# Expert weights in pairs of slabs with 16 KB per partition, and late small loads, in a four-layer block kernel

## The reference

```python
def first_block(x, c, ...):                 # d = 1024, s = 512
    mod = silu(c) @ w_ada + b_ada           # six vectors of 1024
    h = rmsnorm(x) * (1 + sc1) + sh1
    u_f, q, k, v = split(h @ w_in)          # fourier part, 8 query heads, 2 key heads
    y_f = fourier_mix(u_f)                  # 2-D FFT, real part, per-head matrix
    y_a = windowed_gqa(rmsnorm(q), rmsnorm(k), v, rel_bias, sink)
    x = x + g1 * (concat(y_f, y_a) @ w_out)
    h2 = rmsnorm(x) * (1 + sc2) + sh2
    return x + g2 * expert_choice_moe(h2)   # 16 experts, 64 tokens each

def expert_choice_moe(h, w_router, w_gate, w_up, w_down):
    aff = softmax(h @ w_router)
    g, idx = top_k(aff.T, 64)               # each expert picks its tokens
    y = (silu(xin @ w_gate) * (xin @ w_up)) @ w_down   # all 1024 x 1024, per expert
    return scatter_add(g * y, idx)
```

## Time and profile before

| | |
|---|---|
| median of 3 runs | 2066.1 us (2063.94 to 2067.38) |
| the profiled execution | 2064.61 us, span 2062.8 us |
| PE busy | 1986.6 us, 96% of the span |
| DVE, ACT, POOL busy | 906.0, 703.9, 14.0 us |
| mean granted TensorE clock | 0.987 of 2.4 GHz |
| moved by DMA | 344.13 MB, of which the experts' weights are 201 MB |

### The profile page before, as it was taken

One profiled execution on the slowest core, in us unless ns is written; L12 is line 12 of the kernel. 1 busy time (PEld: TensorE's weight loads), 2 busy tenths in 40 slices (PEclk: granted clock), 3 DMA queues, 4 the chain that ended last, 5 costly groups with the idle time before them and its releaser, 6 DMA issues.

```text
span 2062.8 us, 23302 instructions
## 1 busy us (share of the span) xinstructions
PE 1986.6 (96%) x9639; PEld 1310.7 (64%) x9639; DVE 906.0 (44%) x1371; ACT 703.9 (34%) x1171; POOL 14.0 (1%) x28
## 2 busy tenths in 40 slices
PE   5999999999999899999999999999998899999999
PEld 4755543333333257775488887877787568888787
DVE  3474132211111145463266666335545447666433
ACT  4354211111111042473333333235443544333323
POOL 1000000000000000000000000000000000000000
PEclk9999999999999999999999999999999999999999
DMA  9459259999999961400233322221212014333221
GB/s 316 149 191 300 80 229 421 422 421 421 421 421 421 421 198 33 143 1 17 65 82 102 101 84 101 93 92 62 82 62 62 1 41 123 90 95 102 84 80 41
DMA packets 180844, 344.13 MB, mean 167 GB/s; under 512 B 21275, under 2 KB 143755, under 8 KB 152963
## 3 DMA queue, kind: packets, MB, share of 16 engines
q1 hardware_dynamic: 179120, 340.46, 45.7%
q0 software_dynamic: 944, 1.91, 0.5%
q10 hardware_dynamic: 675, 0.27, 0.1%
HBM read 340.50 MB, written 2.11 MB: 166 GB/s over the span
## 4 chain that ended last, share of the span: by engine, by line
PE 82%; DMA 12%; DVE 4%; ACT 2%; issue 1%; ACTq 0%; SPq 0%; DVEq 0%
PE bank L1953 21%; PE bank L1215 13%; PE bank L1970 12%; PE bank L1768 6%; DMA ring<-in_w_gate 4%; PE bank L1787 3%; PE bank L1679 3%; PE bank L763 3%; PE bank L1167 2%; PE bank L807 2%; PE bank L784 2%; PE bank L1155 1%; DMA const<-in_w_gate 1%; DMA hT<-in_w_gate 1%; DMA moe_high<-in_w_gate 1%; DMA work<-in_w_gate 1%
## 5 line engine op out<-in xcount | busy, mean ns | idle before, releaser
L507 DVE TENSOR_TENSOR ring_low<-ring,w_high 128x2048 fp32r<-128x2048 f32 (+1 forms) x87 | 198.4, 2282 | 119.7 <-ACT w_high L500 119.7
L1953 PE MATMUL bank<-h_high,ring_low 128*128 128x512 f32 x640 | 249.7, 390 | 0.0
L500 ACT ACTIVATE w_high<-ring 128x2048 fp32r<-128x2048 f32 (+1 forms) x87 | 165.4, 1903 | 242.1 <-PE bank L1953 174.0
L1953 PE MATMUL bank<-low_ff,w_high 128*128 128x512 f32 x608 | 238.3, 392 | 0.0
L1953 PE MATMUL bank<-h_high,w_high 128*128 128x512 f32 x608 | 236.5, 389 | 0.0
L1970 PE MATMUL bank<-ff_split,w_high 128*128 128x512 f32 x704 | 222.0, 395 | 1.6 <-DVE work L2607 1.6
L1970 PEld LDWEIGHTS bank<-ff_split,w_high 128*128 128x128 f32 x704 | 132.0, 188 | 36.2 <-DVE work L2607 2.4
L1970 PE MATMUL bank<-ff_split,ring_low 128*128 128x512 f32 x352 | 139.0, 395 | 0.0
L1953 PEld LDWEIGHTS bank<-h_high,ring_low 128*128 128x128 f32 x640 | 120.3, 188 | 26.5
L1953 PEld LDWEIGHTS bank<-h_high,w_high 128*128 128x128 f32 x608 | 114.1, 188 | 25.2
L1953 PEld LDWEIGHTS bank<-low_ff,w_high 128*128 128x128 f32 x608 | 114.1, 188 | 24.5
(11 more groups left out here) (392 smaller groups left out, 3344.4 us busy)
## 6 DMA issues: line engine op xcount, KB each, us to landing
ring<-in_ffn_w_up SPq DMA_DIRECT2D x88, 512.0 KB, 5.1
ring<-in_w_down SPq DMA_DIRECT2D x29, 1024.0 KB, 26.4
ring<-in_w_up SPq DMA_DIRECT2D x27, 1024.0 KB, 25.1
ring<-in_w_gate SPq DMA_DIRECT2D x27, 1024.0 KB, 21.8
ring<-in_ffn_w_down SPq DMA_DIRECT2D x22, 1024.0 KB, 4.9
ring<-in_w_ada SPq DMA_DIRECT2D x18, 1024.0 KB, 7.0
ring<-in_od_w_in SPq DMA_DIRECT2D x12, 1024.0 KB, 5.2
moe_high<-in_w_gate SPq DMA_DIRECT2D x10, 1024.0 KB, 24.6
```

Source lines behind the costliest of these rows:

```text
L500: act.activation(high_of(n, words), slab_view(g)[:, 0:words], ACT.Copy).then_inc(sem("split_high"), 1)
L507: dve.tensor_tensor(ring_low[:, slot_of(g), 0:words], slab_view(g)[:, 0:words], high_of(n, words).bitcast(F32), ALU.subtract).then_inc(sem ...
L1953: mm = pe.matmul(bank[n % 6][:, :], st[k], mv[k], start=(k == 0), stop=(k == len(st) - 1))
```

## The change

Expert weights are loaded two slabs at a time. A pair holds rows 4p to 4p + 3 of a block of 512 rows on partition p, 16 KB that adjoin in memory, in two adjacent places, with one DMA of 2 MB. There are now sixteen places in eight pairs: `const` and `norm_area` give two each. A pair is loaded when both its places are free; TensorE waits for it at its first slab. The order within an expert becomes gate, gate, up, up. ScalarE's Silu begins behind the last gate slab, and VectorE's product waits for the last up slab itself. The turns step by four columns instead of two (L1705, L1748, L1778), and L1705 has 32 products instead of 8.

To make room, `const` is shortened: the bases of the fourier part and the bias buckets lie at first where the causal mask and the rotary tables will be, and these three (768 KB) are loaded behind the second slab of the even layer. The cosine table is complete in memory, and ScalarE's three copies of it (L2130) go. `x_rows` lies over `y_high`, `act_T` over `act_e`.

Small loads move: the late vector groups from ScalarE's queue to SyncE's behind the tables, their turns behind tile 6 of the input projection; GpSimd clears its areas and loads `w_fourier` and `rel_bias` first, behind the last slab of the first third of `w_ada`, then gains and lambdas. The lambdas are computed behind the sums of the fourier part, their Exp stands behind tile 8.

```diff
         SB_CONST = CONST_AT["causal"][0]
-        assert SB_CONST >= CONST_AT["rel"][0] + SLAB and SB_CONST + 10 * P + 2 * P <= t["const"].shape[1]
+        CONST_W = CONST_AT["rel"][0] + 2 * SLAB
+        assert SB_CONST == CONST_AT["rel"][0] + SLAB and SB_CONST + 10 * P + 2 * P <= CONST_W
...
-        const = sb("const", [P, t["const"].shape[1]])
+        const = sb("const", [P, CONST_W])
...
             at = 4 * (n - H_SLOTS[0])
             return hT[:, at:at + 4, :].rearrange("p a b -> p (a b)")
+
+        def two_places(n):
+            if n < RING:
+                return ring[:, n:n + 2, :].rearrange("p a b -> p (a b)")
+            if n in HIGH_SLOTS:
+                return moe_high[:, :, :].rearrange("p a b -> p (a b)")
+            if n in TAIL_SLOTS:
+                at = MOE_TAIL + SLAB * (n - TAIL_SLOTS[0])
+                return work[:, at:at + 2 * SLAB]
+            if n in CONST_SLOTS:
+                return const[:, MASKS:MASKS + 2 * SLAB]
+            if n in NORM_SLOTS:
+                return norm_area[:, :]
...
         def moe_source(pair, m):
             e, w = PAIR_ORDER[m]
             if w < 8:
-                x = t["w_gate"] if w % 2 == 0 else t["w_up"]
-                k0 = w // 2
+                x, k0 = (t["w_gate"], t["w_up"])[w // 2 % 2], w // 4
             else:
-                x = t["w_down"]
-                k0 = w - 8
-            return x[0][2 * pair + e, k0 * 2 * P:(k0 + 1) * 2 * P, :].rearrange("(p k) n -> p k n", p=P)
+                x, k0 = t["w_down"], (w - 8) // 2
+            return x[0][2 * pair + e, k0 * 4 * P:(k0 + 1) * 4 * P, :].rearrange("(p k) n -> p k n", p=P)
         GU_BANK = (3, 0)
         SCATTER_BANK = (2, 7)
         GATHER_BANK = (2, 4)
         X_BANK = (2, 1)
         moe_at.append(MOE_0)
-        ring_freed = [(MOE_0 - EARLY + j) % RING for j in range(RING)]
-        moe_slots += [*HIGH_SLOTS, CONST_SLOT, *TAIL_SLOTS[2:], *ring_freed, *H_SLOTS, NORM_SLOT]
+        ring_freed = sorted(range(0, RING, 2), key=lambda n: max(slot_holds[n:n + 2]))
+        moe_slots += [*HIGH_SLOTS, *CONST_SLOTS, *TAIL_SLOTS[2:], *(n + x for n in ring_freed for x in range(2)), *H_SLOTS, *NORM_SLOTS]
         moe_w = []
         for m in range(MOE_N):
             v = slab_view(len(slabs)).rearrange("p (k n) -> p k n", k=2)
-            moe_w.append((plan([(v, moe_source(m // 24, m % 24))], sem("moe_used"), m + 1), v))
+            both = two_places(slot_of(len(slabs))).rearrange("p (k n) -> p k n", k=4) if m % 2 == 0 else None
+            moe_w.append((plan([] if m % 2 else [(both, moe_source(m // 24, m % 24))], sem("moe_used"), m + 1), v))
         *late_order, LOW_SLOT = sorted(range(RING), key=lambda n: slot_holds[n])
...
             def load(g):
                 pieces, _, _ = slabs[g]
-                if before_in_slot[g] is not None:
-                    _, used, count = slabs[before_in_slot[g]]
-                    sp.wait_ge(used, count)
+                for h in (g, g + 1) if MOE_0 <= g < MOE_0 + MOE_N else (g,):
+                    if before_in_slot[h] is not None:
+                        _, used, count = slabs[before_in_slot[h]]
+                        sp.wait_ge(used, count)
                 for o, i in pieces:
...
             for g in range(0, DT + 2):
                 load(g)
-            for c0, c1 in ((FIRST, MASKS), (MASKS + SLAB, t["const"].shape[1])):
-                sp.dma_start(const[:, c0:c1], t["const"][:, c0:c1]).then_inc(sem("tables_loaded"), 16)
+            front = t["const"].shape[1] - FRONT
+            for a, c, n in ((FIRST, FIRST, MASKS - FIRST), (SB_CONST, FRONT, front)):
+                sp.dma_start(const[:, a:a + n], t["const"][:, c:c + n]).then_inc(sem("tables_loaded"), 16)
+            for g in range(1, len(VEC_GROUPS)):
+                r = 0
+                for name, n, off in VEC_GROUPS[g]:
+                    sp.dma_start(vec_row[r:r + n, g, :], vec_source(name)[off:off + n, :]).then_inc(sem("late_vec_loaded"), 16)
+                    r += n
             for g in range(DT + 2, MOE_0):
                 load(g)
-            for g in range(MOE_0, MOE_0 + MOE_N):
-                if g - MOE_0 < len(moe_slots) and slot_of(g) in HIGH_SLOTS:
+            for g in range(MOE_0, MOE_0 + MOE_N, 2):
+                if g - MOE_0 < len(moe_slots) and slot_of(g) == HIGH_SLOTS[0]:
                     sp.wait_ge(sem("in1_done"), len(in1_tiles))
...
                 if before_in_slot[g] is None and slot_of(g) == H_SLOTS[0]:
                     sp.wait_ge(sem("out1_done"), DT)
-                if before_in_slot[g] is None and slot_of(g) == NORM_SLOT:
+                if before_in_slot[g] is None and slot_of(g) == CONST_SLOTS[0]:
+
+                    sp.wait_ge(sem("chan_done"), 1)
+                if before_in_slot[g] is None and slot_of(g) == NORM_SLOTS[0]:
                     sp.wait_ge(*wide_step("ffn", "sums"))
                 load(g)
             for g in range(MOE_0 + MOE_N, len(slabs)):
+                if g == MOE_0 + MOE_N + 2:
+
+                    sp.wait_ge(sem("moe_used"), slot_holds[CONST_SLOTS[1]] - MOE_0 + 1)
+                    sp.dma_start(const[:, SB_CONST:SB_CONST + 3 * S], t["const"][:, SB_CONST:SB_CONST + 3 * S])\
+                      .then_inc(sem("tables_loaded"), 16)
                 if g == ffn_w[0][0][0][0]:
                     sp.wait_ge(sem("evin_done"), len(evin_tiles))
...
         @block.gpsimd
         def _(pool):
+            pool.wait_ge(sem("ada_used"), DT)
+            pool.memset(chan_w, 0.0).then_inc(sem("pool_cleared"), 1)
+            pool.wait_ge(sem("pool_cleared"), 1)
+            pool.memset(relb[N_BUCKETS:N_BUCKETS + 1], 1.0).then_inc(sem("pool_cleared"), 1)
+            pool.dma_start(wf[0:HD].rearrange("c (g d) -> c g d", g=8), t["w_fourier"][0].rearrange("g c d -> c g d"))\
+                .then_inc(sem("wf_loaded"), 16)
+            pool.dma_start(relb[0:N_BUCKETS], t["rel_bias"]).then_inc(sem("relb_loaded"), 16)
             for o, name in ((qg_col, "q_norm_g"), (kg_col, "k_norm_g")):
                 for b in range(2):
                     pool.dma_start(o[HD * b:HD * b + HD], t[name].rearrange("a n -> n a")).then_inc(sem("gain_loaded"), 16)
...
             pool.dma_start(sink_b, t["sink"].to_broadcast([P, N_HEADS])).then_inc(sem("gain_loaded"), 16)
             for i, name in enumerate(("ev_lam_q1_2", "ev_lam_k1_2", "ev_lam_q2_2", "ev_lam_k2_2")):
                 pool.dma_start(lam_b[:, i, :], t[name].to_broadcast([P, HD])).then_inc(sem("lam_loaded"), 16)
-
-            pool.wait_ge(sem("ada_used"), len(TAIL_SLOTS))
-            pool.memset(chan_w, 0.0).then_inc(sem("pool_cleared"), 1)
-            pool.wait_ge(sem("pool_cleared"), 1)
-            pool.memset(relb[N_BUCKETS:N_BUCKETS + 1], 1.0).then_inc(sem("pool_cleared"), 1)
-            pool.dma_start(wf[0:HD].rearrange("c (g d) -> c g d", g=8), t["w_fourier"][0].rearrange("g c d -> c g d"))\
-                .then_inc(sem("wf_loaded"), 16)
-            pool.dma_start(relb[0:N_BUCKETS], t["rel_bias"]).then_inc(sem("relb_loaded"), 16)
...
             def turn_vec(g):
                 n = sum(x[1] for x in VEC_GROUPS[g])
-                pe.transpose(bank[1 + g][:, 0:n], vec_row[0:n, g, :], ident[0:n, 0:n]).then_inc(sem("vec_turned"), 1)
+                o = bank[6][:, P * (g - 1):P * (g - 1) + n] if g else bank[1][:, 0:n]
+                pe.transpose(o, vec_row[0:n, g, :], ident[0:n, 0:n]).then_inc(sem("vec_turned"), 1)
...
                 ada_slab(m)
                 if m == 0:
                     wide_spread(pe, "mix")
-                if m == 1:
+            ada_turn(0)
+
+            def in1_after(i):
+                if i == 6:
                     pe.wait_ge(sem("late_vec_loaded"), 16 * sum(len(g) for g in VEC_GROUPS[1:]))
-                    pe.wait_ge(sem("x_copied"), DT)
                     for g in range(1, len(VEC_GROUPS)):
                         turn_vec(g)
-            ada_turn(0)
-
-            def in1_after(i):
                 if i == 4:
...
             token_sums(pe, "ffn", True)
             turn_x(DT - 1)
             for n, x in enumerate((gain2, mod[:, 24:24 + DT])):
-                for j in range(2):
-                    for h in range(2):
-                        mm = pe.matmul(bank[0][HD * h:HD * h + HD, DT * n + j:DT * n + DT:2], ident[:, j::2], x[:, h:DT:2], start=True,
+                for j in range(4):
+                    for h in range(4):
...
                 pe.wait_ge(sem("xrow_copied"), 2 * i + j + 1)
                 for k in range(4):
-                    c0 = S * j + HALF * (k // 2) + k % 2
-                    mm = pe.transpose(bank[X_BANK[j]][:, P * k:P * k + P], x_rows[:, c0:c0 + HALF - 1:2], ident)
+                    mm = pe.transpose(bank[X_BANK[j]][:, P * k:P * k + P], x_rows[:, S * j + k:S * j + S:4], ident)
                 mm.then_inc(sem("x_turned_e"), 1)
...
             def gate_up_pe(i, e, w):
                 g, v = moe_w[24 * i + 8 * e + w]
```

(45 more changed lines are left out.)

89 lines of the change are left out of this document (53 added, 36 removed).

## The result

The changed kernel took 2049.6 us (median of 4 runs, 2048.0 to 2050.6) beside 2066.5 of the kernel before (4 runs): ratio 0.992, 95% interval 0.9902 to 0.9937. Two later measurements of the same kernel, on other occasions, gave 2051.0 beside 2063.2 (0.994, 0.9927 to 0.9953) and 2050.9 beside 2063.5 (0.994, 0.9926 to 0.9954). So it is faster by 12 to 17 us, 0.6 to 0.8%. The forecast was 8.8, with 2057.3 and a range down to 2052.5: the sign is right, the size is too small, and the time lies outside the range. The profiled execution took 2048.03 us, its span is 2046.2 us.

What follows compares the result with a forecast made beforehand. The expert stage was taken to end when the last of 192 slabs lands, its stream saturated at 421 GB/s. Terms summed to -8.8 from 2064.6, so 2055.8, or 2057.3 for the median; range 2052.5 to 2064.5.

Steps and rivals of the forecast that it cites:

- Two more places, minus 5.0: Expert stage: 16 slabs instead of 14 loaded beforehand leave 176 instead of 178 for the saturated stream, 5.0 us less.
- Restart in pairs, plus 1.7: Expert stage's first reload waits until TensorE is through two slabs instead of one, 1.7 us more.
- Tail, plus 1.9: End of the expert stage: TensorE has two slabs to work off behind the last landing, not one, 1.9 us more.
- Rows of 16 KB, minus 5.3: Expert weight stream: 16 KB rows run 1.2% faster than 8 KB rows, 5.3 us less, bounds 0 and 6.2.
- Start, minus 3.0: First microseconds: without the small loads the last w_ada slab and b_fourier come earlier and TensorE follows, 3.0 us less.
- four vector turns, plus 0.6: Input projection: the late vectors' four turns and copies stand behind tile 6, where TensorE is the chain, 0.6 us more.
- lambdas, minus 0.4: Near 55 us: with the lambdas off the path, the first copy of the input projection starts about 0.4 us earlier.
- The upper bound, 3.8: The most that the start was said to gain, 3.8 us.
- the rival that the start doesn't follow: The chain hangs on ScalarE's own queue of loads, so the start gains less: plus 2.4, 2059.7 us; chance 0.12.
- Gain turns by four, plus 0.7: Routing: L1705's 64 matmuls, at 35 ns each, hold up ScalarE's small copy, 0.7 us more, within 0.2 to 2.0.
- At nothing: Moved vector loads, gains, lambdas' loads, dropped cosine copies, the 768 KB table reload and pair waits were said to cost nothing.
- TensorE as the bound through stride four: Expert stage: turns reading by stride four take three times as long and use up TensorE's 13 us reserve, 2072 us; chance 0.06.

Runs made afterwards that it cites:

- places_14: The changed kernel without its last two places (the norm area), 14 as before: 2055.2 us, ratio to before 0.9962.
- tail_single: The changed kernel with the stage's last two pairs loaded as four single slabs, each with its own wait: 2049.4 us beside 2065.4 of before, 0.9921.
- rows_4k: The changed kernel with each pair loaded as four transfers of 4 KB rows: 2069.3 us beside 2065.4 of before, 1.0020.
- start_only: The kernel before with all edits of the start and none of the expert stage: 2058.7 us beside 2063.5 of before, 0.9975.
- before_again: The kernel before once more, unchanged, one run: 2068.5 us.
- pool_early: The changed kernel with GpSimd's ten small loads back at the start, vector groups still late: 2055.2 us beside 2064.4 of before, 0.9954.
- pool_twice: The changed kernel with GpSimd's ten small loads at the start and the same ten again into an unused place: 2057.3 us, ratio to before 0.9959.
- ends_single: The changed kernel with the first reload and the last pair loaded as single slabs: 2049.7 us beside 2064.4 of before, 0.993.
- before_pool_late: The kernel before with only GpSimd's ten small loads moved behind the last slab of w_ada: 2059.3 us beside 2064.4 of before, 0.9978.
- rows_8k: The changed kernel with each pair loaded as two transfers of 8 KB rows: 2056.5 us, ratio to before 0.9964.

## Why the prediction was right in sign and too small

*Two more places, minus 5.0*: right, 4.6 by places_14.

*Restart in pairs, plus 1.7*: right. The first reload came 3.67 us behind the first gate matmul, before 1.91. *Tail, plus 1.9*: 1.7 (3.68 against 1.96 us behind the last landing); tail_single gave back 1.3 of it.

*Rows of 16 KB, minus 5.3*: right mechanism, mis-sized. It is 5.5 us in the medians and 6.0 between first reload and last landing. The line through 1 KB and 8 KB said 1.4% and measured 1.4%; taking 1.2%, "below it, since both lie on one side", cost the 0.7 us. This term is mis-sized too, though by less. By rows_4k the line holds at a third size, so 421 GB/s was no limit of bytes although the share read 1.01. The Trainium skill (DMA: Bandwidth & Descriptors, Why small descriptors are slow) names a mechanism of this kind, a fixed cost for each packet, but the estimate from its 3 cycles is 0.6% here and 1.75% between 4 and 16 KB, where 1.4% and 4.4% were measured.

*Start, minus 3.0* with *four vector turns, plus 0.6* and *lambdas, minus 0.4*: this is the step that failed. The sum is minus 2.8; measured are 4.9 us on the first gate matmul (mean of 283.05 and 285.80 against that of 279.66, 279.24 and 279.70), 4.8 in start_only's median, and 4.5 to 5.2 on the landing of the last slab of w_ada (35.07 and 35.79 against a mean of 30.59). With the low stretch near 92 us on both sides or on neither, the first gate matmul gained more: 6.3 us from before_again to the changed kernel's mean, and 5.2 from the first profile of before to the 277.8 and 277.9 of rows_4k and tail_single, which have the same start. Within it the turns were nearly right (0.48 us), the lambdas are 0.9 to 1.4 instead of 0.4 in the chain and not to be told in the time.

What was wrong is "They hold 0.173 x 16 = 2.8 us of all engines", read as what the w_ada stream loses. With GpSimd's ten and ScalarE's six loads SyncE's queue moved 1.63 MB less in 16 us, 3.9 us at 420 GB/s, and its share was 22 points lower (3.5 us), not 17. With GpSimd's ten alone (pool_early) they held 16.5%, 2.6 us, and SyncE's queue moved 1.47 MB less, 3.5 us. The difference is made of what their own share doesn't show: engines stand idle from 10 to 15 us (share 0.93 against 1.01), ScalarE's queue held 1.3 points more, and in its own time SyncE's queue moved 0.36 instead of 0.386 MB per us of all engines. The upper bound, 3.8, was made from the same share and so was too low too. TensorE followed in full: b_fourier came 5.2 us earlier, and the rival that the start doesn't follow is out. Why ten small loads slow the others beyond what they hold is not settled. It isn't only the first microseconds: the second ten of pool_twice held 1.4 us, and the last slab of w_ada landed 2.6 later.

*Gain turns by four, plus 0.7*: wrong, nothing. Thirty-two of the matmuls take 0.66 us, some 20 ns each and not 35. And the step named the wrong wait: ScalarE's copy (L2193) stands behind a table load of 1.28 us and the copy of h_tok, until 253.9, while the matmuls are through at 253.3. From the table load to this copy it is 1.88 us in both kernels. I had read its start as the end of the wait for L1705 and not looked at what ran on ScalarE ahead of it.

*At nothing*: nothing large. The first profile seemed to show 5.7 us more gained behind the stage; the repeats put this down to the clock. From L1155 on before took 1322.0 and 1322.3 us, from L1180 on the changed kernel took 1316.3, 1324.6 and 1319.4.

The sum as measured: start minus 4.9, restart plus 1.8, places minus 4.6, rows minus 6.0, tail plus 1.7, gain turns nothing: minus 12.0, against 12.2 and 12.6 in the two measurements with more runs. With these 5.2 to 6.3 for the start it is 12.3 to 13.4. The 16.9 of the first had some 4 us of scatter in it (its four runs of before lay at 2063.9 to 2067.4, the 62 later ones have medians of 2063.2 to 2065.4). The clock carries a part of that: its four runs of the changed kernel had a mean of 0.989, the later ones 0.988; for its runs of before only one clock is known, 0.987. So the true miss is 3 to 4 us and not 8: some 2 from the start, 0.7 each from the rows and the gain turns.

*The rivals.* TensorE as the bound through stride four is out: the four turns (L1817) take no longer than with stride two. In the groups of lines, a weight load has a median of 212 ns and a turn 285 ns, 209 and 283 before:

```profile
L1817 PEld LDWEIGHTS bank<-const,work x64: 195/212/220, 298.6 to 712.7; 128*128 128x128 f32 x64
L1817 PE MATMUL bank<-const,work x64: 283/285/386, 298.6 to 712.8; 128*128 128x128 f32 x64
```

The rule of the Trainium skill (Advanced Engine Details and Errata, SBUF Cachelines) that spoke for it isn't borne out for TensorE's reads. TensorE did come nearer to being the bound, as worked out. Its stage now ends at 724.14. Its own work would end near 711.4, by the prediction's sum from the changed kernel's rows (a pair's down projections end at 551.36, less 4 x 55.33, plus 7 x 55.33, less 6). So it has some 13 us in hand, as forecast, where before it had 20.

## What to carry to other kernels

A packet's fixed cost is still in a stream of 8 KB rows that reads as saturated: fit a line through two row sizes of the trace and believe it. The share that a foreign queue holds was a lower bound for what the main stream lost beside it (2.6 against 3.5 us, 1.4 against 1.6), so small loads that nobody needs yet leave the first microseconds; read the bytes that the main queue moves there, not the share of the other. And before a wait is priced, look at what its own engine does in front of it; a gain of four runs is only as good as their clocks.

## What the hardware showed unexpectedly

A row costs an engine 9 to 10 ns beside its bytes, from 4 to 16 KB (409, 421, 428 GB/s) and with the 1 KB of the earlier trace rows too: four sizes on one line. A stream of 1 MB loads that restarts after 20 idle us is slow in some profiles and not in others, though the engines are busy either way (share 0.83 or more). In the 6 us that begin 2 us behind the first reload it ran at 360 GB/s in start_only, at 330 and 347 in before_again and at 352 and 393 in ends_single, but at 412 and 404 in the first profile of the same kernel as before_again, and at 421 and 423 in before_pool_late. The kernels with loads of 2 MB ran at 399 or more there, and so did rows_8k, whose two loads left together. What makes the difference was not tried. Matmuls with two columns behind weight loads of 32 columns go at one per 20 ns. The lower clock behind 900 us comes and goes between executions of one kernel, at a cost of up to 8 us (1316.3 and 1324.6), and so does the stretch near 92 us, at a cost of 1.5.
